# Mixer: the recurrence split between the next inverse and the projections of the step behind it

## What is computed

```
def step(state, inp):
    r_t, w_t, k_t, v_t, kk_t, a_t = inp
    sa = jnp.einsum('bhvk,bhk->bhv', state, kk_t)
    state = (state * w_t[:, :, None, :]
             - sa[..., None] * (kk_t * a_t)[:, :, None, :]
             + v_t[..., None] * k_t[:, :, None, :])
    y = jnp.einsum('bhvk,bhk->bhv', state, r_t)
    return state, y
```

## Time and profile before

| | |
|---|---|
| median of 3 runs | 4946.42 us (4941.43 to 4950.04) |
| profiled execution | 4945.55 us, of which the span of instructions 4943.8 us |
| mean granted TensorE clock | 0.973 of 2.4 GHz |
| TensorE busy | 4566.7 us (92%) |
| VectorE, ScalarE, GpSimd busy | 1631.0, 1346.4, 345.4 us |
| DMA | 128 GB/s over the span, 8% of the engines' time in the mixer |

### The profile page before, as it was taken

How to read it: one execution, slowest core, us unless ns; L and a number is a source line. 1 busy time by engine, 2 the same in 40 slices (tenths; PEclk the granted TensorE clock), 3 DMA queues, 4 the chain that set the end, 5 groups by cost and what they waited for, 6 DMA issues and landing times.

```text
span 4943.8 us, 91839 instructions
## 1 busy us (share of the span) xinstructions
PE 4566.7 (92%) x36823; PEld 2450.1 (50%) x36823; DVE 1631.0 (33%) x2946; ACT 1346.4 (27%) x3050; POOL 345.4 (7%) x466
## 2 busy tenths in 40 slices
PE   6999999999999999999999998994999999999992
PEld 4455555555555555555555555453444444444440
DVE  3334334334334334333343343224111111111115
ACT  4123333333333333333333333431111111111115
POOL 0001001001001000000010000000000000000004
PEclk8999999999999999999999999996999999999996
DMA  8101001001001001001001002333788888888887
GB/s 295 50 5 47 11 8 47 10 12 43 10 12 43 10 12 45 9 12 46 8 12 46 8 12 69 107 123 132 281 330 334 339 330 341 333 330 343 331 321 297
DMA packets 252914, 637.61 MB, mean 129 GB/s; under 512 B 11027, under 2 KB 96245, under 8 KB 252533
## 3 DMA queue, kind: packets, MB, share of 16 engines
q1 hardware_dynamic: 238852, 582.26, 32.3%
q0 software_dynamic: 13680, 49.81, 2.6%
HBM read 563.32 MB, written 68.71 MB: 128 GB/s over the span
## 4 chain that ended last, share of the span: by engine, by line
PE 87%; issue 4%; DVE 3%; DMA 2%; ACT 1%; SPq 1%; POOL 0%; DVEq 0%; POOLq 0%; ACTq 0%
PE bank L892 36%; PE bank L1218 18%; PE bank L1237 9%; PE bank L1106 5%; PE duo L1017 3%; PE duo L1004 2%; PE duo L1006 1%; PE duo L1207 1%; DMA yb<-y_s,dix 1%; PE bank L949 1%; ACT xs L1264 1%; PE bank L933 1%; PE duo L829 1%; PE duo L986 1%; PE bank L921 1%
## 5 line engine op out<-in xcount | busy, mean ns | idle before, releaser
L892 PE MATMUL bank<-hT,w 128*128 (+1 forms) x4096 | 1788.3, 593 | 0.0
L892 PEld LDWEIGHTS bank<-hT,w 128*128 128x128 f32 x4096 | 776.3, 190 | 991.0 <-issue 991.0
L1218 PE MATMUL bank<-WI,xT 128*128 128x512 f32 x2016 | 877.6, 593 | 2.4 <-DVE xT L2055 2.4
L1218 PEld LDWEIGHTS bank<-WI,xT 128*128 128x128 f32 x2016 | 378.9, 190 | 456.1 <-issue 456.1
L1237 PE MATMUL bank<-WO,aT 128*128 128x512 f32 x1008 | 443.1, 592 | 1.0 <-DVE ysb L2072 1.0
L1264 ACT ACT_TABLE_LOAD x268 | 343.8, 1283 | 21.1 <-DVE ub L1807 14.3
L2061 DVE TENSOR_TENSOR gsig<-bank,gsig 128x512 f32<-128x512 f32 x63 | 43.6, 692 | 847.4 <-ACT gsig L1264 847.4
L1237 PEld LDWEIGHTS bank<-WO,aT 128*128 128x128 f32 x1008 | 186.7, 190 | 212.6 <-issue 211.4
L1264 ACT ACTIVATE gsig<-bank 128x512 f32<-128x512 f32 x63 | 37.6, 597 | 827.6 <-PE bank L1218 827.6
L659 POOL TENSOR_TENSOR Tm<-Tm,idents 128x512 f32<-128x512 f32 x32 | 40.6, 1269 | 2826.3 <-DVE Tm L1848 2826.3
L1106 PE MATMUL bank<-wo,mT 128*128 128x512 f32 x512 | 233.6, 603 | 0.0
(11 more groups left out here) (340 smaller groups left out, 5369.0 us busy)
## 6 DMA issues: line engine op xcount, KB each, us to landing
WI<-in_w_expert_in_dram SPq DMA_DIRECT2D x63, 4096.0 KB, 17.2
WO<-in_w_expert_out_dram SPq DMA_DIRECT2D x63, 2048.0 KB, 7.9
w<-in_w_in_dram SPq DMA_DIRECT2D x64, 512.0 KB, 3.9
y_s<-ysb SPq DMA_DIRECT2D x63, 512.0 KB, 17.8
adaw<-in_w_ada_dram SPq DMA_DIRECT2D x12, 2048.0 KB, 12.9
xt<-in_x_dram SPq DMA_DIRECT2D x16, 512.0 KB, 9.0
WAc<-rank_s SPq DMA_DIRECT2D x32, 256.0 KB, 3.4
GDc<-rank_s SPq DMA_DIRECT2D x32, 256.0 KB, 3.2
```

Source lines behind the costliest of these rows:

```text
L892: ins = mm(PJ[j % 2][:, :], w[:, j, k, :], hT[:, k, ds(group(i) * G, G)], start=k == 0, stop=k == KT - 1)
L1218: ins = mm(GU[j][:, :], xT[:, s, k, :], WI[:, s, k, j * DE:j * DE + DE], start=k == 0, stop=k == KT - 1)
```

## The change

The list `SCHED` now holds 12 hops, chunks 0 to 3 (`HALF_NC` is 4): two in each level of the inverse, one before and one behind the transposes, and none around T and Q. Chunks 4 to 7 of the recurrence of step i - 2 go into `head(i)`, between single matmuls of `proj(i, 0)` and `proj(i, 1)`: six behind k = 1 to 6 of projection 0, six behind k = 2 to 7 of projection 1. Since projections fill `PJ` then, these chunks use `X_LAST`, two banks of the inverse, and their first `seq_ahead` waits until all products of step i - 1's inverse are evacuated (`gram_evac`, `tok_copied`). ScalarE's copies and VectorE's state updates move with them, and `copy_y` and `y_sum` move from the end of a step to behind projection 1 of the next. At the end, chunks 4 to 7 of step 30 now run behind the loop with an output matmul behind each hop, and the eight chunks of step 31 follow with two output matmuls each, behind x and u. The arithmetic is the same; nothing is added or left out.

```diff
-def level(lv, hops):
-    return [("Z", lv, (0, 1)), hops[0], ("TR", lv - 1, (0, 1)), hops[1], ("T", lv, (0, 1)), hops[2],
-            ("Q", lv, (0, 1)), hops[3]]
+HALF_NC = NC // 2
 def sched_plan():
-    n = [(kind, c) for c in range(NC) for kind in ("x", "u", "sy")]
-    plan = [("L", 0, (0, 1)), n[0], ("LT", 0, (0,)), n[1], ("LT", 0, (1,)), n[2], ("GK", 0, (0,)), n[3],
-            ("GK", 0, (1,)), n[4]]
-    plan += level(1, [n[5], None, n[6], n[7]])
-    for lv in range(2, 5):
-        plan += level(lv, n[4 * lv:4 * lv + 4])
-    plan += [("Z", 5, (0, 1)), n[20], ("TR", 4, (0, 1)), n[21], ("TR", 5, (0, 1)), n[22], ("Q", 5, (0, 1)), n[23]]
-    return [("hop" if x[0] in ("x", "u", "sy") else "use",) + x for x in plan if x]
+    n = iter([(kind, c) for c in range(HALF_NC) for kind in ("x", "u", "sy")])
+    plan = [("L", 0, (0, 1)), ("LT", 0, (0,)), next(n), ("LT", 0, (1,)), ("GK", 0, (0,)), next(n), ("GK", 0, (1,))]
+    for lv in range(1, 6):
+        plan += [("Z", lv, (0, 1)), next(n), ("TR", lv - 1, (0, 1)), next(n)]
+        plan += [("T", lv, (0, 1)) if lv < 5 else ("TR", 5, (0, 1)), ("Q", lv, (0, 1))]
+    return [("hop" if x[0] in ("x", "u", "sy") else "use",) + x for x in plan]
...
-            def proj(i, j):
+            def proj(i, j, hops={}, p=0):
                 pe.wait_ge(w_in_sem[j], tile_no(i) * 16 + 16)
                 if j >= 2:
...
                 elif not first(i):
                     wait_released(j + 6, i - 1)
                     if prior2(i) is not None:
-                        pe.wait_ge(S["S_updated"], (i - 1) * NC)
+                        pe.wait_ge(S["S_updated"], (i - 2) * NC + HALF_NC)
                 for k in range(KT):
                     ins = mm(PJ[j % 2][:, :], w[:, j, k, :], hT[:, k, ds(group(i) * G, G)],
                              start=k == 0, stop=k == KT - 1)
-                ins.then_inc(S["proj_done"], 1)
+                    if k == KT - 1:
+                        ins.then_inc(S["proj_done"], 1)
+                    if k in hops:
+                        name, c = hops[k]
+                        {"x": seq_x, "u": seq_u, "sy": seq_sy}[name](i - 2, c, p, X_LAST)
             def seq_ahead(q, c, p, xb=XB):
+                if c == HALF_NC and not (isinstance(q, int) and q == STEPS - 1):
+                    pe.wait_ge(S["gram_evac"], q * NDV + 2 * NDV)
+                    pe.wait_ge(S["tok_copied"], q * NTK + 2 * NTK)
                 if c == 0:
-                    if isinstance(q, int) and q == STEPS - 1:
-                        pe.wait_ge(S["yT_summed"], q)
-                    else:
+                    if xb is XB:
                         pe.wait_ge(S["gates"], q * 2 + 4)
                     pe.wait_ge(S["gram_evac"], q * NDV + NDV)
                     pe.wait_ge(S["tok_copied"], q * NTK + NTK)
                     pe.wait_ge(S["Q_seeded"], q + 1)
+                if c in (0, HALF_NC):
                     pe.sem_inc(S["pair_go"])
                 k, a = divmod(c, 2)
                 h = 1 - a
...
                     ins = mm(yb[h][HALF[h], cs], St[HALF[h], c % 2, :], AR[p][HALF[h], c, 0:HD],
                              start=h != a, stop=True)
                 ins.then_inc(S["y_done"], 1)
-                if c + 1 < NC:
+                if c + 1 < NC and not (xb is XB and c + 1 == HALF_NC):
                     seq_ahead(q, c + 1, p, xb)
...
-            def head(i):
+            def head(i, p):
                 zdec(i)
                 zaaa(i)
-                proj(i, 0)
-                proj(i, 1)
+                if prior2(i) is None:
+                    proj(i, 0)
+                    proj(i, 1)
+                else:
+                    seq_ahead(i - 2, HALF_NC, p, X_LAST)
+                    late = [(kind, c) for c in range(HALF_NC, NC) for kind in ("x", "u", "sy")]
+                    proj(i, 0, dict(zip(range(1, 7), late[:6])), p)
+                    proj(i, 1, dict(zip(range(2, 8), late[6:])), p)
...
-            pe.wait_ge(S["S_updated"], (STEPS - 1) * NC)
-            pe.wait_ge(S["yT_summed"], STEPS - 1)
+            pe.wait_ge(S["S_updated"], (STEPS - 2) * NC + HALF_NC)
             pe.wait_ge(S["wo_in"], 32)
-            parts = [(0, 0, j, k) for j in range(2) for k in range(KT)] + [(1, 1, 0, k) for k in range(KT)]
+            parts = iter([(0, 0, j, k) for j in range(2) for k in range(KT)]
+                         + [(1, 1, j, k) for j in range(2) for k in range(KT)][:2 * KT - 4])
+            seq_ahead(STEPS - 2, HALF_NC, 0, X_LAST)
+            for c in range(HALF_NC, NC):
+                seq_x(STEPS - 2, c, 0, X_LAST)
+                out_mm(*next(parts))
+                seq_u(STEPS - 2, c, 0, X_LAST)
+                out_mm(*next(parts))
+                seq_sy(STEPS - 2, c, 0, X_LAST)
+                out_mm(*next(parts))
             seq_ahead(STEPS - 1, 0, 1, X_LAST)
             for c in range(NC):
                 seq_x(STEPS - 1, c, 1, X_LAST)
-                out_mm(*parts[3 * c])
+                out_mm(*next(parts))
                 seq_u(STEPS - 1, c, 1, X_LAST)
-                if c == 0:
+                if c == 1:
                     centred(STEPS - 2, M1)
-                if c == 1:
+                if c == 2:
                     variance(STEPS - 2, M1)
-                out_mm(*parts[3 * c + 1])
+                if c == 6:
+                    pe.wait_ge(S["rs_step"], STEPS * 2 - 3)
+                out_mm(*next(parts))
                 seq_sy(STEPS - 1, c, 1, X_LAST, Y_LAST)
-                out_mm(*parts[3 * c + 2])
-            pe.wait_ge(S["rs_step"], STEPS * 2 - 3)
-            for k in range(2):
-                out_mm(1, 1, 1, k)
             pe.wait_ge(S["S_updated"], STEPS * NC)
             centred(STEPS - 1, SA)
-            for k in range(2, 4):
+            for k in range(4, 6):
                 out_mm(1, 1, 1, k)
             variance(STEPS - 1, SB)
-            for k in range(4, KT):
+            for k in range(6, KT):
                 out_mm(1, 1, 1, k)
...
+                if q2 is not None:
+                    for c in range(HALF_NC, HALF_NC + 2):
+                        copy_begun(q2, c, X_LAST)
+                        copy_x(q2, c, X_LAST)
+                        copy_u(q2, c, X_LAST)
                 scaled(0, Q_MUK)
                 act.wait_ge(S["shifted"], i * 3 + 1)
                 if not first(i):
                     act.wait_ge(S["branch"], i * 3 - 2)
                 fn(sq[:, :], kt[:, :], ACT.Square, scale=par[:, Q_KK:Q_KK + 1]).then_inc(S["ksq_ready"], 1)
+                if q2 is not None:
+                    for c in range(HALF_NC + 2, NC):
+                        copy_begun(q2, c, X_LAST)
+                        copy_x(q2, c, X_LAST)
+                        copy_u(q2, c, X_LAST)
                 scaled(1, Q_MUR)
+                if q2 is not None:
+                    copy_y(q2)
...
-                if q is not None:
-                    copy_y(q)
...
+                if q2 is not None:
+                    for c in range(HALF_NC, HALF_NC + 2):
+                        S_update(q2, c, p, X_LAST)
                 mixed(i, 0, kt, Q_OMK)
                 dve.wait_ge(S["sg_ready"], i + 1)
                 if not first(i):
...
                 dve.wait_ge(S["km_step"], i * 2 + 1)
                 dve.wait_ge(S["shifted"], i * 3 + 1)
                 V.tensor_tensor(km[:, :], km[:, :], kt[:, :], ALU.mult).then_inc(S["km_step"], 1)
+                if q2 is not None:
+                    for c in range(HALF_NC + 2, NC):
+                        S_update(q2, c, p, X_LAST)
                 mixed(i, 1, rt, Q_OMR)
                 dve.wait_ge(S["shifted"], i * 3 + 2)
                 dve.wait_ge(S["km_step"], i * 2 + 2)
                 dve.wait_ge(S["cum_done"], i + 1)
                 V.tensor_tensor(rk[:, :], rt[:, :], km[:, :], ALU.mult).then_inc(S["rk_ready"], 1)
+                if q2 is not None:
+                    y_sum(q2)
...
-                if q is not None:
-                    y_sum(q)
```

More of the change, by code:

```diff
@@ L71 @@
 NUSE = len(PLAN)
-assert [x[1:] for x in SCHED if x[0] == "hop"] == [(k, c) for c in range(NC) for k in ("x", "u", "sy")]
+assert [x[1:] for x in SCHED if x[0] == "hop"] == [(k, c) for c in range(HALF_NC)
+                                                         for k in ("x", "u", "sy")]
 def pair_of(u):
@@ L1087, in _ @@
             pe.wait_ge(S["cleared"], 5)
-            head(0)
+            head(0, 0)
             tail(0, 0)
-            head(1)
+            head(1, 1)
             tail(1, 1)
-            head(2)
+            head(2, 0)
             with pe.Fori(1, STEPS // 2 - 1) as h:
                 tail(h * 2, 0)
-                head(h * 2 + 1)
+                head(h * 2 + 1, 1)
                 tail(h * 2 + 1, 1)
-                head(h * 2 + 2)
+                head(h * 2 + 2, 0)
             tail(STEPS - 2, 0)
-            head(STEPS - 1)
+            head(STEPS - 1, 1)
             tail(STEPS - 1, 1)
@@ L1422, in step @@
```

(20 more changed lines are left out.)

## The result

The changed kernel takes 5171.95 us (median of 4 runs, 5166.26 to 5175.96), and the kernel before on the same chip 4948.23 us: a ratio of 1.0456, 95% interval 1.0441 to 1.0470. It is slower, as forecast, but by 224 us and not by 90; the time lies 82 us above the upper end of the range. One run of experiment e6 took 10421.51 us, twice its three others, and the median leaves it aside.

The account below looks back on a forecast made before the run. TensorE's own stream was taken as the bound. 30 heads at 8.5 us more dense stretch and 5.5 less inverse (+90), the 31st inverse -5.5 and the end +6.0 gave +90.5 us: 5037 us, range 4985 to 5090.

Parts of the forecast that it names:

- What bounds the kernel: Whole loop: TensorE's own stream is 87% of the chain of waits; anything put into the dense stretch lengthens it.
- The price of the hops in the projections: Dense stretch, projections 0 and 1: four chunks cost 8.24 us, 8.5 us taken with look-ahead and new wait.
- three edges of 0.2 us: Projections, each chunk: from matmul to hop 1.06 us in place of 0.86, at each of three edges.
- What moves on other engines and costs nothing: ScalarE and VectorE around the dense stretch: sigmoids end near 3.4 us, chunk 4's copy is ready with 0.4 us cover.
- rival 2: Dense stretch: ScalarE or VectorE is late, some 1.5 us a step, +45, 5082 us; chance 0.10.
- What leaves the inverse: Inverse: moving 12 of 24 hops out saves 5.5 us a step, within bounds of 3.8 and 7.5 us.
- The term for the start: Inverse, start with level 1: a state update and x more behind VectorE's evacuations add 0.65 us.
- The clock: Dense stretch and inverse: the granted clock is 1.00 (2.4 GHz) in both.
- The end: Behind the loop: recurrence and output matmuls grow from 44.0 to 51.8 us, with 0.6 us of wait; +6.0 us.
- rival 4: Projections: hops hide in weight slack, so the kernel is faster, 4929 us or near 4870, below 1.31 us a chunk; chance 0.05.

Follow-up runs that it names:

- e6: Changed kernel with ScalarE's copies of chunks 4 and 5 before the sigmoids, six hops at the inverse's start, transposes' copy before the hop's copy: 5034.40 us, 1.0179.
- e4: Kernel before, plus one needless 64x64 matmul at each of the 12 hop places in projections 0 and 1 and the evacuation waits: 5156.81 us, 1.0430.
- e8: Kernel before, plus a needless full 128x128 matmul of 64 columns at each of the 12 hop places and the evacuation waits: 5071.86 us, 1.0259.
- e10: Kernel before, plus 12 needless 64x64 matmuls all at one place in projection 0 and the evacuation waits: 5047.90 us, 1.0195.
- e1: Changed kernel with ScalarE's copies of chunks 4 and 5 ahead of the parameter wait, carry copy and two sigmoids: 5118.31 us, 1.035.
- e3: Changed kernel with the same 12 hops in the inverse, the first six back at its start around L, LT, GK and Z1: 5090.21 us, 1.0295.
- e2: Changed kernel with ScalarE copying the transposes (tok) ahead of the hop's copy: 5170.34 us, 1.0452.
- e5: Changed kernel with ScalarE's copies of chunks 4 and 5 ahead of the sigmoids and the first six hops at the inverse's start: 5036.59 us, 1.0186.
- e7: Changed kernel split at chunk 6: 18 hops in the inverse, six at its start, chunks 6 and 7 in projection 0, ScalarE's copies before the sigmoids: 5002.99 us, 1.0121.

## Why the prediction was right and wrong

**What bounds the kernel: right.** TensorE's stream did set the time, and each microsecond added to the dense stretch came back 30 times.

**The price of the hops in the projections: right, and small by a little.** The bare price was taken at 8.24 us for four chunks from the earlier trace rows, 8.5 us with what belongs to it. The dense stretches without a wait are 69.9 us, 8.8 more than the 61.1 of the same steps before. Over 29 steps the 0.3 us are 8 us. In rows of the same form the trace of before held nearly the whole answer. That a place and not the columns is paid for, I had put down to three edges of 0.2 us; e4, e8 and e10 make it 0.46 us a place.

**"What moves on other engines and costs nothing": this step failed.** It put the parameters 1.0 us after `zdec` and the sigmoids' end near 3.4. That holds in one of two steps. In the other VectorE pauses 2.60 us at the start of its loop, and the sigmoids end 5.9 us after `zdec` (1712.48). The pause was in the trace of before and I had read it away: I put the late parameters (1516.76) down to `y_sum` in front of them and did not look at the other step, where 3.80 us of issue stood before them. It was rival 2, priced at 1.5 us a step; the wait was 1.8 to 2.1 us in every second, which is 0.9 us a step. The larger part was in no rival: the clock that falls behind the wait, up to 4.8 us in such a step. Together they are 2.0 us a step (71.89 against 69.90 over steps 2 to 30), 58 us. e1 gave back 54.

**"What leaves the inverse": this step failed too.** A saving of 5.5 us was forecast and 3.8 us called the least; it was 3.3. Over 30 inverses the missing 2.2 us are 67 us. The term for the start is where it begins. I took +0.65 us over step 0 for the start and level 1. The wait in front of the first transposes (1.83 us in step 0) is contained in those 22.89 us, and it came back at the same length with only three hops in front of it. In the inverse that begins at 1582.72, at clock 0.94, L to the first T takes 7.36 us (7.0 forecast), and that T to the next Z 3.12 us in place of 1.68. In the one that begins at 1778.40, at clock 1.00, the second is 2.16 us, so about 1 us of it goes with the half clock. From the second Z to the fifth the first of them takes 12.3 us; the other takes 14.3, with the issue time shown above. So it is the slow clock early or issue time later (in one inverse both), and the sum had neither. With the hops placed as in e3 the inverse saved 6.0 us and all 30 were at clock 1.00: the plan of the start is what cost the 2.75 us. By what share wait, clock and issue time make them up stays open. That Q waits behind ScalarE's hop copy I had missed; e2 and e6 show that to cost next to nothing, because issue time takes its place.

**The clock.** The prediction took 1.00 from one step of the earlier trace rows. The last row has 0.99: in the kernel before, 8 of the 30 inverses have a fall, behind waits of 0.7 to 1.4 us most of which are issue time. A price for it could have been asked from there.

**The end: about 6 us short.** From the `zdec` of step 31 to the end of the span it is 1960.5 us before and 1975.8 after, +15.3; less 8.5 for that dense stretch this leaves +6.8, where -5.5 + 6.0 = +0.5 were forecast. The traces show two parts of it. The last inverse, from L to its last Q, went from 38.20 to 36.12 us, 2.1 less and not 5.5, with issue time of 3.05, 2.25 and 2.72 us in front of Z. And TensorE now waits 2.90 us for `y_sum` of step 31, ahead of its `centred` at 3359.66, where 0.6 us of wait were allowed.

Together, for the profiled executions: 90.5 forecast + 8 + 58 + 67 + 6 give some 230 us, the difference of the spans. That e5, with both repairs and no other change, is 5036.6 us and so meets the forecast is in part luck: up to the `zdec` of step 31 it has 9 us less than was worked out, and behind it 10 us more.

**The other rivals.** The faster one (rival 4) needed under 1.31 us a chunk in the projections; it was 2.1, as in the earlier trace rows. The Trainium skill's main page ("Trainium Kernel Development and Optimization", Performance Expectations) would judge by MFU and the LDWEIGHTS share; the dense stretch had 26.46 of 60.73 us of weight loads and yet no room, and here the measurement decides against reading that share as room. The range was too narrow because it held the rivals one by one: two moderate misses of the same sign had no place in it.

## What to carry to other kernels

A gap that nobody fills can cost more than its length: in this kernel 1.8 to 2.1 us of idle TensorE in a stream without holes were followed in 8 of 14 steps by 3 to 10 us at half clock, which cost up to 4.8 us more. So price a new wait with the slow time behind it, and place the few fillers that are left where the longest hole is. In a stretch that has holes of its own the fall need not cost anything (the inverse of step 0, 22.89 us without and 22.52 with it). Before filling one engine's dense stream with small work, count the places where its kind of tile changes and not the columns: a place cost 0.46 us, without a change of tile 0.23, a further small matmul there 0.12. And when work is put behind an instruction that "has slack", look at that instruction in every step of the loop body and not in one.

## What the runs showed that was not expected

- VectorE pauses for 2.4 to 3.8 us once per pass of its loop, in front of the first instruction, and every second step inherits it.
- In the dense stretch the granted clock fell behind waits, and not because the stream is broken up: with 12 hops in the projections and no wait for xs there, the dense stretches of e1 and e5 from step 1 on are all at 1.00. The same wait of 1.8 to 2.1 us led to a fall in the dense stretch in some steps and in others not (71.8 us at 1.00), and e7 and the kernel before have falls behind issue time of 0.7 to 1.8 us. What decides it, the runs don't show.
- The inverses of the changed kernel that keep clock 1.00 are longer than those whose clock falls (28.4 to 28.9 us against 26.4 to 27.7 us, but for one), by issue time in front of Z.
- Needless matmuls in the projections made the inverse behind them 1.2 to 1.6 us longer, as issue time.
- Removing 40.8 us of waits for tok brought 36 us of issue time and no gain (e2), so a wait in the list is worth at most what the next limit leaves.
